# A six-layer network on one core: conditioning products placed between the products of four output projections

## The reference, cut to what matters

```python
def adaln(cond, w_mod, b_mod):
    return jnp.split(jax.nn.silu(cond) @ w_mod + b_mod, 6, axis=-1)
```

## Time and profile before

| | us |
|---|---|
| median of three runs | 3682.59 |
| lowest, highest | 3681.91, 3683.28 |
| the profiled execution, its own time | 3689.55 |
| its span, from first to last instruction | 3687.8 |

### The profile page before, as it was taken

The page is one execution under the profiler, slowest core; times in us unless marked ns, Lnnn a source line. Parts: engine busy times, 40 slices in busy tenths (PEclk is TensorE's granted clock), DMA queues, the critical chain, the costliest instruction groups (busy, mean ns, idle before and its releaser), DMA issues. The chain is left out here.

```text
span 3687.8 us, 41084 instructions
## 1 busy us (share of the span) xinstructions
PE 3315.2 (90%) x16240; PEld 2607.2 (71%) x16240; DVE 1830.3 (50%) x2739; ACT 1220.0 (33%) x2115; POOL 83.6 (2%) x89
## 2 busy tenths in 40 slices
PE   7998997988899879778899988889999989989997
PEld 5866665656687634578788855668888867867876
DVE  4556696544564656683524389342222246543333
ACT  3245323345334512563212222232121233632222
POOL 0000000000100000000000012000000000000000
PEclk9999999999999989899999999899999999999999
DMA  4222111201222121692111021211111111122221
GB/s 147 85 59 73 69 57 46 80 27 55 96 82 57 63 84 80 263 341 81 39 54 69 25 101 56 80 46 57 69 57 69 46 64 32 51 78 91 91 91 57
DMA packets 49237, 292.01 MB, mean 79 GB/s; under 512 B 7496, under 2 KB 7752, under 8 KB 17913
## 3 DMA queue, kind: packets, MB, share of 16 engines
q1 hardware_dynamic: 47032, 283.05, 21.6%
q0 software_dynamic: 2048, 6.82, 0.6%
HBM read 262.84 MB, written 14.68 MB: 75 GB/s over the span
## 5 line engine op out<-in xcount | busy, mean ns | idle before, releaser
L407 PE MATMUL bank<-high,slot_high 128*128 128x512 f32 (+1 forms) x3344 | 1241.5, 371 | 132.3 <-DVE low L331 89.2
L408 PE MATMUL bank<-low,slot_high 128*128 128x512 f32 (+1 forms) x3344 | 1229.0, 368 | 0.0
L409 PE MATMUL bank<-high,slot_low 128*128 128x512 f32 (+1 forms) x3344 | 1226.0, 367 | 0.0
L387 DVE TENSOR_TENSOR slot_low<-slot,slot_high 128x2048 fp32r<-128x2048 f32 (+1 forms) x172 | 389.8, 2266 | 1190.9 <-ACT slot_high L381 1190.8
L407 PEld LDWEIGHTS bank<-high,slot_high 128*128 128x128 f32 x3344 | 636.2, 190 | 270.9 <-issue 127.1
L381 ACT ACTIVATE slot_high<-slot 128x2048 fp32r<-128x2048 f32 (+1 forms) x172 | 325.7, 1894 | 1369.7 <-PE bank L409 1162.2
L409 PEld LDWEIGHTS bank<-high,slot_low 128*128 128x128 f32 x3344 | 635.6, 190 | 112.5
L408 PEld LDWEIGHTS bank<-low,slot_high 128*128 128x128 f32 x3344 | 636.3, 190 | 109.8 <-issue 4.6
L931 DVE TENSOR_REDUCE peak<-bank 128x1 f32<-128x128 f32 (+2 forms) x224 | 108.9, 506 | 139.6 <-PE bank L1060 53.2
L983 ACT ACTIVATE prob<-bank,peak_bias 128x128 f32<-128x128 f32 (+2 forms) x224 | 119.8, 542 | 69.8 <-DVE peak_bias L939 69.6
L2336 PE MATMUL bank<-mod_high,cond_halves 128*128 128x256 f32 x384 | 102.4, 303 | 32.0 <-DVE mod_low L2363 31.9
(11 more groups left out here) (379 smaller groups left out, 4040.5 us busy)
## 6 DMA issues: line engine op xcount, KB each, us to landing
mod_raw<-in_mod SPq DMA_DIRECT2D x48, 1024.0 KB, 7.2
slot<-in_gu SPq DMA_DIRECT2D x44, 1024.0 KB, 4.8
slot<-in_a_in SPq DMA_DIRECT2D x32, 1024.0 KB, 4.8
slot<-in_e_rest SPq DMA_DIRECT2D x16, 1024.0 KB, 4.8
slot<-in_down SPq DMA_DIRECT2D x16, 1024.0 KB, 4.7
spectra<-f_spectrum SPq DMA_DIRECT2D x12, 1024.0 KB, 3.9
h_spectrum<-spectra SPq DMA_DIRECT2D x12, 1024.0 KB, 4.9
slot<-in_a_out SPq DMA_DIRECT2D x8, 1024.0 KB, 6.1
```

Source lines behind the costliest of these rows:

```text
L387: dve.tensor_tensor(k.slot_low[s][:, 0:n], k.slot[s][:, 0:n], k.slot_high[s][:, 0:n].bitcast(F32), ALU.subtract).then_inc(k.low[s], 1)
L407: pe.matmul(out, wh, xh, start=kt == 0, stop=False)
L408: pe.matmul(out, wh, xl, start=False, stop=False)
L409: mm = pe.matmul(out, wl, xh, start=False, stop=kt == self.kt - 1)
```

## The change

A new class, `Conditioning`, takes a quarter of the modulation's product into each of the four output projections: the 12 chunks of half a layer, as 24 halves of 512 KB. They go through four buffers, which in the attention stages are the value tiles that are no longer needed. Nothing is split: the chunk is multiplied as it is, in float32, by the two vectors in float32. The place still moves by four columns with each chunk, and two of the four hold something. The stationary operand has 48 columns. A half is a group of four products of 256 columns, into bank 5. The groups stand behind chosen steps of a slot (`PLACES`: four in the first slot, all in its second half, seven in the second and third, six in the last). SP fetches the next phase's weights behind the 16th half. At the end of the block ACT copies the 48 rows, and SP stores them in DRAM and waits for this.

The modulation's block keeps the small products, the bias, the gains and the statistics; SP reads the stored rows of the two layers, and POOL clears what lies beyond them. The small products now come ahead of the statistics on PE. The activation of the vectors moves to the first block.

```diff
+        self.silu = self.sb("silu_cond", 16)
...
-    def multiply(self, k, pe, u, moving, ready=None, behind=None):
+    def multiply(self, k, pe, u, moving, ready=None, behind=None, beside=None):
...
+                        if beside:
+                            beside(pe, 2 * i + s, t * self.kt + kt)
                 if behind:
                     behind(i, s)
 
-        if behind:
+        if behind or beside:
             for i in range(self.pairs):
                 turn(i)
...
+class Conditioning:
...
+    PLACES = (9, 11, 13, 15), (1, 3, 6, 8, 10, 12, 14), (1, 3, 6, 8, 10, 12, 14), (1, 3, 6, 8, 10, 12)
+    FIRST = 0, 4, 11, 18
+    HALVES, RAW, WIDTH, ROWS = 24, 4, KT // 2 * 256, 48
+    FETCH_AT = 15
+
+    def __init__(self, k, ctx, w, rows, layer, part, raw=None):
+        self.k, self.weight, self.layer, self.part = k, w["mod"], layer, part
+        self.stored_rows = rows[layer, part * self.ROWS:(part + 1) * self.ROWS, :]
+        raw = raw if raw is not None else k.sb("mod_raw", self.RAW * self.WIDTH, ctx)
+        self.raw = [raw[:, x * self.WIDTH:(x + 1) * self.WIDTH] for x in range(self.RAW)]
+        self.place = self.ROWS - 4
+        self.strip = k.sb("cond_strip", KT * (self.place + self.ROWS), ctx)
+        self.wide = self.strip[:, :].rearrange("p (t c) -> p t c", c=self.place + self.ROWS)
+        self.row = k.sb("mod_row", 256, ctx)
+        self.used, self.strip_made, self.copied, self.stored = (k.named(n) for n in (
+            "mod_used", "mod_strip", "mod_copied", "mod_stored"))
+        self.landed = [k.named(f"mod_landed{x}") for x in range(self.RAW)]
+
+    def pool(self, pool):
+        pool.memset(self.strip[:, :], 0.0).then_inc(self.strip_made.sem, 1)
+        pool.wait_ge(self.strip_made.sem, self.strip_made.at(1))
+        pool.tensor_copy(self.wide[:, :, self.place:self.place + 2], self.k.silu[:, :].rearrange("p (t c) -> p t c", c=2))\
+            .then_inc(self.strip_made.sem, 1)
+
+    def load(self, sp, fetch):
+        for n in range(self.HALVES):
+            if n >= self.RAW:
+                sp.wait_ge(self.used.sem, self.used.at(n - self.RAW + 1))
+            chunk, half = self.layer * 24 + self.part * 12 + n // 2, n % 2
+            sp.dma_start(self.raw[n % self.RAW], self.weight[chunk, :, half * self.WIDTH:(half + 1) * self.WIDTH])\
+              .then_inc(self.landed[n % self.RAW].sem, 16)
+            if n == self.FETCH_AT:
+                fetch()
+        sp.wait_ge(self.copied.sem, self.copied.at(1))
+        sp.dma_start(self.stored_rows, self.row[0:self.ROWS, :]).then_inc(self.stored.sem, 16)
+        sp.wait_ge(self.stored.sem, self.stored.at(16))
+
+    def tensor(self, pe, slot, step):
+        if step not in self.PLACES[slot]:
+            return
+        n = self.FIRST[slot] + self.PLACES[slot].index(step)
+        if n == 0:
+            pe.wait_ge(self.strip_made.sem, self.strip_made.at(2))
+            pe.wait_ge(self.k.drained[5], self.free)
+        landed = self.landed[n % self.RAW]
+        pe.wait_ge(landed.sem, landed.at(16 * (n // self.RAW + 1)))
+        at = self.place - 4 * (n // 2)
+        out = self.k.ps[5][0:self.ROWS, 0:256]
+        for x in range(KT // 2):
+            still = self.wide[:, n % 2 * (KT // 2) + x, at:at + self.ROWS]
+            a = slice(x * 256, (x + 1) * 256)
+            mm = pe.matmul(out, still, self.raw[n % self.RAW][:, a], start=n == x == 0,
+                           stop=n == self.HALVES - 1 and x == KT // 2 - 1)
+        mm.then_inc(self.used.sem, 1)
+
+    def end_tensor(self, pe):
+        pe.wait_ge(self.used.sem, self.used.at(self.HALVES))
+        pe.sem_inc(self.k.filled[5], 1)
+
+    def take_rows(self, act):
+        act.wait_ge(self.used.sem, self.used.at(self.HALVES))
+        act.activation(self.row[0:self.ROWS, :], self.k.ps[5][0:self.ROWS, 0:256], ACT.Copy)\
+           .then_inc(self.k.drained[5], 1)
+        act.wait_ge(self.k.drained[5], self.free + 1)
+        act.sem_inc(self.copied.sem, 1)
+
...
-    loaded = k.named("loaded")
+    loaded, vec_in, lit = k.named("loaded"), k.named("vectors_loaded"), k.named("condition_ready")
...
-            sp.dma_start(k.vec[:, :], src["vec"]).then_inc(loaded.sem, 16)
+            sp.dma_start(k.vec[:, :], src["vec"]).then_inc(vec_in.sem, 16)
-            sp.wait_ge(loaded.sem, 48)
+            sp.wait_ge(loaded.sem, 32)
+
+        @block.scalar
+        def _(act):
+            act.wait_ge(vec_in.sem, 16)
+            act.activation(k.silu[:, :], k.vec[:, VEC["cond"]:VEC["cond"] + 16], ACT.Silu).then_inc(lit.sem, 1)
...
-        output_a(k, w, j, lambda_init, O, ssq, G, out, follow)
+        output_a(k, w, j, lambda_init, O, ssq, G, out, follow, (w, rows, j, j, V))
...
+        mod = Conditioning(k, ctx, *side) if side else None
+        if mod:
+            mod.free = k.uses.free(5, 2)
...
-            if follow:
+            if mod:
+                mod.load(sp, lambda: follow and follow.fetch(k, sp, u[0]))
+            elif follow:
                 follow.fetch(k, sp, u[0])
...
             drive(k, act, u[1], "take_high", [(res.phase, tail.scalar(act) if tail else None)], True, follow=follow)
+            if mod:
+                mod.take_rows(act)
...
             turn.tensor(k, pe, u[3], ready)
-            res.phase.multiply(k, pe, u[3], op.moving(LATENT), turn.ready(k, pe))
+            res.phase.multiply(k, pe, u[3], op.moving(LATENT), turn.ready(k, pe), beside=mod.tensor if mod else None)
             if tail:
                 tail.tensor(pe, u[3])
+            if mod:
+                mod.end_tensor(pe)
...
+                if mod:
+                    mod.pool(pool)
+                if tail:
+                    tail.pool(pool)
...
+        mod = Conditioning(k, ctx, w, rows, 0, 1)
+        mod.free = k.uses.free(5)
...
-        project_heads_split(k, O, None, G, Residual(out), follow=follow)
+        project_heads_split(k, O, None, G, Residual(out), follow=follow, side=(w, rows, 1, 0, V))
...
-def modulation(k, w, mod, gain, first):
+def modulation(k, rows_in, mod, gain, first):
...
-            def turn(i):
-                for s in range(S):
-                    if not isinstance(i, int):
-                        sp.wait_ge(low_made.sem, low_made.at(i * S + (s + 1 - S)))
-                    sp.dma_start(raw[s], w["mod"][bass.ds(i * S + s, 1), :, :].rearrange("a p n -> (a p) n"))\
-                      .then_inc(landed[s].sem, 16)
-
-            turn(0)
-            loop(sp, turns, turn, first=1)
+            for layer in range(2):
+                sp.dma_start(rows[layer][0:96, :], rows_in[layer, :, :]).then_inc(rows_read[layer].sem, 16)
             first.fetch(k, sp, u[0])
             close(u[0])
...
-            act.activation(cond[:, :], k.vec[:, VEC["cond"]:VEC["cond"] + 16], ACT.Silu).then_inc(lit.sem, 1)
-            act.wait_ge(lit.sem, lit.at(1))
...
-                    act.activation(high[s], raw[s], ACT.Copy).then_inc(high_made.sem, 1)
...
             stats.square(k, act)
-            turn(0)
             stats.take_roots(k, act, u[1])
-            loop(act, turns, turn, first=1)
+            close(u[1])
+
+        @block.gpsimd
+        def _(pool):
             for layer in range(2):
...
-                act.wait_ge(k.filled[layer], u[1].full(layer))
-                act.activation(rows[layer][:, :], k.ps[layer][:, 0:256], ACT.Copy).then_inc(k.drained[layer], 1)
...
-            stats.tensor(k, pe, u[2].copy())
-            pe.wait_ge(halved.sem, halved.at(2))
+            pe.wait_ge(k.drained[2], u[2].free(2))
+            pe.wait_ge(cleared.sem, cleared.at(2))
             for layer in range(2):
-                pe.wait_ge(k.drained[layer], u[2].free(layer))
-                for chunk in range(24):
-                    n, s, at = layer * 24 + chunk, chunk % S, place - rows_per * chunk
-                    pe.wait_ge(low_made.sem, low_made.at(n + 1))
-                    for kt in range(KT):
-                        a = slice(kt * 256, (kt + 1) * 256)
-                        pe.matmul(k.ps[layer][:, 0:256], wide[:, kt, at:at + P], high[s][:, a],
-                                  start=chunk == kt == 0, stop=False)
-                        mm = pe.matmul(k.ps[layer][:, 0:256], wide[:, kt, at:at + P], low[s][:, a],
-                                       start=False, stop=chunk == 23 and kt == KT - 1)
-                    mm.then_inc(used.sem, 1)
-                pe.wait_ge(used.sem, used.at(24 * layer + 24))
-                pe.sem_inc(k.filled[layer], 1)
-            pe.wait_ge(k.drained[2], u[2].free(2))
-            for layer in range(2):
-                pe.wait_ge(k.drained[layer], u[2].full(layer))
+                pe.wait_ge(rows_read[layer].sem, rows_read[layer].at(16))
                 for t in range(2):
                     at = (2 * layer + t) * 48
                     mm = pe.matmul(k.ps[2][:, at:at + 48], rows[layer][:, t * P:(t + 1) * P], k.c("halves", 48),
```

(10 more changed lines are left out.)

## The result

The changed kernel takes 3745.01 us (median of 4 runs, 3742.78 to 3747.55), the kernel before 3682.25 (4 runs, 3680.11 to 3683.28). The ratio is **1.0171 [1.0154, 1.0189]**: 62.8 us slower. The forecast was slower by 33, 3704 to 3736: the sign is right, the size is not, and the time lies outside the range. The profiled execution of after took 3743.58 us (span 3741.8), 1.4 under its median; that of before lay 7.0 to 7.3 over its own. So the two traces differ by 54.0 us and the medians by 62.8.

A forecast was written before the change was run, and what follows sets the result against it. PE bounds the kernel, except in the modulation's block, which transfers bound. Products 165.7 + block ends 4.8 - old block 136.3 - first load 1.3 = +32.9 us on 3682.6, rounded 3716; range 3704 to 3736.

The forecast's parts named there:

- The price of a full product: Output projections: a full-precision product of 256 columns is two records of 0.2158 us, 0.4316 us; 384 products cost 165.7 us.
- The loads lie under the products anyway: Output projections: loads of the 48-column stationary operand are hidden under the products, so their length adds nothing.
- Nothing is left over for the changes: Output projections: changing between split and full products costs zero, read from a full product of 512 columns among split ones.
- Rival 2: Output projections: a bubble at each of 96 groups, the unmet-wait pitch paid twice; 19 us more, 3735; chance 9%.
- The block that goes: Modulation's block: shrinks from 160.1 to 23.8 us, saving 136.3 us (bounds 135 to 139).
- Ends of three blocks: Ends of the first three projections: row copy and awaited store delay the next block 1.6 us each, 4.8 in all.
- First ACT table load: First block: ACT's Silu load moves into its wait for input, a 1.28 us load falls away; 1.3 us saved.
- Transfers: Output projections: halves land within the 11.6 us allowed, 157 GB/s, some 200 with the next weights; cost zero.
- slots: Output projections: 23.2 us for the second and third slot, 21.5 for the last, PE without idle time.
- rivals 1, 3 and 4: Half-price products, 3633, 3%; late transfers, 3744, 4%; change not doing what it says, each 10 us giving 3726, 3%.

## Why the prediction failed, step by step

- **The price of a full product: right.** The pitch inside a group is 0.216 us, a group in the kernel of 128 columns 1.72. That kernel lies 33.9 us above the kernel before; the forecast's sum was 32.9. Without the narrow operand the sum holds within about 1 us.
- **"The loads lie under the products anyway": wrong, and this is the step that failed.** I looked at the length of the 48-column load and not at whether it may begin early. It does not, at either end of a group: 0.32 us that the sum put at nothing, 31 us for 96, and with them 32.9 + 31 = 64 against the 62.8 measured.
- **"Nothing is left over for the changes"** was read well but answers another question: both products there have 128 columns. What I needed was an operand of half size between full ones, and the trace of before has one, at full clock, in the third mixer (L2073 with 64 rows, L2090 with 64 rows and 64 columns; PEld rows, with the products around them):

```profile
751.18 0.39 PE L2058 MATMUL bank<-c_low_high,c_up_low 128*128 128x512 f32 x1
751.50 0.29 PEld L2073 LDWEIGHTS bank<-slot,con 64*128 64x128 f32 x2 [0.35 <-issue]
751.50 1.12 PE L2073 MATMUL bank<-slot,con 64*128 64x512 f32 x2
752.55 0.19 PEld L2090 LDWEIGHTS bank<-c_krope,con 64*64 64x64 f32 x2 [0.76 <-issue]
752.55 1.07 PE L2090 MATMUL bank<-c_krope,con 64*64 64x512 f32 x2
753.55 0.19 PEld L2056 LDWEIGHTS bank<-c_low_high,c_up_high 128*128 128x128 f32 x1 [0.81 <-issue]
753.55 0.50 PE L2056 MATMUL bank<-c_low_high,c_up_high 128*128 128x512 f32 x1
...
754.12 0.42 PEld L2073 LDWEIGHTS bank<-slot,con 128*128 128x128 f32 x2
754.35 0.59 PE L2073 MATMUL bank<-slot,con 128*128 128x512 f32 x1
```

  The same signs: pitch 0.32 at the head (751.18 to 751.50), "issue" before the load, and loads that begin with their products. Three microseconds later L2073 with a 128 x 128 operand has its load 0.23 us ahead. From 751.50 to 753.55 two full products of 512 columns, four records, take 2.05 us; at 0.2158 per 256 columns they would take 1.73. With the 0.09 at the head and the 0.11 behind (L2056 to L2057, 753.55 to 753.89), the three changes of shape in these rows cost 0.5 us, so for the two of a group they would have given some 0.35 (an estimate).
- **Rival 2 named the right sign**, a late first split product, with 9%. Its mechanism, the unmet wait of the earlier trace rows, was the wrong one, and its 0.2 us per group was too small. The range took its upper end from it and so missed as well: its 3736 is 9 us short. A bubble "at every group" with no row that excludes it for a 48-column operand deserved more than 9%.
- **The block that goes: right.** 136.5 us saved, forecast 136.3. The rows landed at 2.1 us (2.5 expected), the statistics took 13.3 (13.6). The sum that gives 23.4 us before the block's end has two slips: its terms (17.2, 1.0 and 4.96) make 23.2, and 1660.57 is the end of the gains on DVE (L2383), not of the reciprocals. Neither matters to the result.
- **Ends of three blocks: right in kind, half in size.** From ACT's last square to the next block it is 2.98 us instead of 2.08 (378.63 to 380.71 in the earlier trace rows), 0.9 later and not 1.6:

```profile
423.97 0.63 ACT L730 ACTIVATE whole<-X 128x512 f32<-128x512 f32 x1 [11.07 <-DVE X L1446]
...
424.94 0.34 SPq L797 DMA_DIRECT2D mod_rows<-mod_row  x1
426.95 0.35 SPq L350 DMA_DIRECT2D slot<-in_b_in_ab  x1
```

  The store is through in 2.0 us, all of it; I had added 0.2 to it and 0.3 behind it. In the last stage it is covered, as told: the next block begins 1.39 us behind PE's last product (1498.06 to 1499.45), as before.
- **First ACT table load: half right.** It is gone, and PE's first sum starts 1.23 us earlier (13.98 for 15.21 in the earlier trace rows), but ACT's work on the first slot only 0.57 (20.43 for 21.00), so the 1.3 was too much.
- **Transfers, slots, rivals 1, 3 and 4: as told**, except that the slots are longer by 0.32 per group: 152 GB/s, landing 3.7 us, two records per product.
- What is left of the 54.0 us between the traces: the first mixer is 3.5 us shorter up to its projection (the table load explains 0.6 to 1.2 of it), the last mixer 2.5, the filters 5.2 (a mean clock of 0.88 before, 0.92 after), and all behind the modulation's block is 2.8 longer. Apart from the start of the first block nothing was changed in these.

## What to carry to other kernels

Before a product of another shape is put between full ones, look in the trace for whether the loads on either side of such a shape begin ahead of their products, and count the changes of shape, not the products. A stationary operand of 48 or 64 columns among ones of 128 cost 0.32 us for each insertion here, and padding it to 72 or more cost nothing. And a product that is moved from a transfer-bound stage to a PE-bound one pays its full PE price there, so make it cheap first: in split form the same move was a gain of 24 us.

## What the runs showed of the hardware beyond that

The loads differ in length with their width (119 to 123 ns for 48 columns, 132 to 137 for 64, 141 to 144 for 72, 187 to 194 for 128), and from 72 to 128 columns the times stay within 3713 to 3717 us. An idle time of 2.76 us of PE was followed by 2.2 us at the lower clock level (0.50), one of 2.69 in the third mixer was not (1.00). Where the clock falls, this is a second price of such a wait: the eight split products of the group took 1.87 us (372.31 to 374.18) in place of 0.94.
